# Hybrid decoder step on one Trainium2 core: the last two expert turns' rows added by TensorE, other rows combined while the experts run, rows dealt out over partitions

## What is computed

```python
m_in, mo_p, q1p, q2p, kr_p, vr_p = mixer_inputs(xp, norm_mix[l], w_in[l], b_gates[l])   # h @ w_in, gates among it
...
xp = xp + mixer_output(hm_p, mo_p, a_p, head_norm_m[l], head_norm_da[l], lam_init, w_out[l], xp.dtype)
...
# moe_ffn: the best of 4 groups, then the best 2 of its 8 experts
gates = jnp.sum(jax.nn.one_hot(expert_id, N_EXPERTS, dtype=jnp.float32) * top_p[..., None], axis=1)
y = jnp.zeros((N, h.shape[1]), jnp.float32)
for e in range(N_EXPERTS):
    act = jax.nn.silu(h @ w_gate[e]) * (h @ w_up[e])
    y = y + gates[:, e:e + 1] * (act @ w_down[e]).astype(jnp.float32)
...
y_prompt = rms_norm(xp, norm_final)[:, N_META:].astype(x_prompt.dtype)
y_sample = rms_norm(xs, norm_final).astype(x_sample.dtype)
```

## Time and profile before

| | us |
|---|---|
| median of 3 runs | 693.38 (692.94 to 696.12) |
| the profiled execution, its own time | 703.3 |
| its span, first to last instruction | 701.5 |
| TensorE busy | 611.1 (87%) |
| DVE busy | 279.6 (40%) |
| ScalarE busy | 139.2 (20%) |
| GpSimd busy | 116.4 (17%) |

### The profile page before, as it was taken

One profiled execution on the slowest core, in us unless ns is written; L12 is line 12 of the kernel. 1 busy time (PEld: TensorE's weight loads), 2 busy tenths in 40 slices (PEclk: granted clock), 3 DMA queues, 4 the chain that ended last, 5 costly groups with the idle time before them and its releaser, 6 DMA issues.

```text
span 701.5 us, 8557 instructions
## 1 busy us (share of the span) xinstructions
PE 611.1 (87%) x3155; PEld 328.6 (47%) x3155; DVE 279.6 (40%) x615; ACT 139.2 (20%) x405; POOL 116.4 (17%) x195
## 2 busy tenths in 40 slices
PE   4999999899898999999989996999999777999700
PEld 2444344445544555555545482555555443555300
DVE  3320068333333452568788778311212111121146
ACT  3111041233323454401131000110101100101111
POOL 2350016110040110101021201011121110211023
PEclk9999999999999999999999966999999998999965
DMA  9643337823030210041084798899999999999674
GB/s 282 197 142 135 121 102 207 280 83 118 4 106 15 73 48 0 1 121 62 1 327 156 238 407 328 359 419 419 419 420 421 419 422 421 420 420 415 250 262 166
DMA packets 49378, 161.45 MB, mean 230 GB/s; under 512 B 16443, under 2 KB 17772, under 8 KB 36664
## 3 DMA queue, kind: packets, MB, share of 16 engines
q1 hardware_dynamic: 39624, 143.67, 52.8%
q0 software_dynamic: 7488, 17.19, 7.4%
q10 hardware_dynamic: 2224, 0.04, 0.2%
HBM read 150.91 MB, written 19.01 MB: 242 GB/s over the span
## 4 chain that ended last, share of the span: by engine, by line
PE 68%; DMA 12%; SPq 7%; DVE 5%; ACT 3%; issue 2%; another core or an unknown queue 2%; POOL 1%; POOLq 0%; DVEq 0%; ACTq 0%
PE bank L1869 11%; PE bank L1872 11%; PE bank L2090 8%; PE bank_p L2140 6%; PE scores L2153 6%; DMA WS<-in_w_down_e 4%; DMA FT<-in_w_down_e 4%; PE bank_t L2140 4%; PE bank_t L1886 3%; SPq L552 3%; SPq L555 2%; DMA WS<-in_w_in 2%; SPq L549 2%; PE bank L2132 2%
## 5 line engine op out<-in xcount | busy, mean ns | idle before, releaser
L1872 PE MATMUL bank<-WS,XHT 128*128 128x512 f32 x192 | 87.4, 601 | 2.0 <-DMA WS<-in_w_in 1.5
L1869 PE MATMUL bank<-XHT,WS 128*128 128x512 f32 x192 | 85.0, 597 | 1.0 <-PE bank_t L1886 1.0
L1869 PEld LDWEIGHTS bank<-XHT,WS 128*128 128x128 f32 x192 | 35.7, 190 | 43.3 <-issue 43.0
L1872 PEld LDWEIGHTS bank<-WS,XHT 128*128 128x128 f32 x192 | 34.8, 190 | 42.5 <-issue 40.4
L2140 PE MATMUL bank_p<-WS,XHT 128*64 128x256 f32 x288 | 45.5, 391 | 5.7 <-DVE XHT L1724 1.5
L915 POOL DMA_INDIRECT out_rows<-MVA,slot_ids x17 | 17.0, 1001 | 188.1 <-DVE MVA L1741 188.1
L2140 PE MATMUL bank_t<-WS,XHT 128*64 128x256 f32 x288 | 43.0, 381 | 1.5 <-DMA FT<-in_w_up_e 0.8
L2140 PEld LDWEIGHTS bank_p<-WS,XHT 128*64 128x64 f32 x288 | 27.7, 141 | 21.0 <-issue 4.3
L1741 DVE COPY MVA<-scores 128x512 f32<-128x512 f32 x17 | 11.8, 692 | 56.9 <-PE scores L2153 56.9
L806 POOL TENSOR_SCALAR rr<-ss 128x1 f32<-128x1 f32 (+3 forms) x25 | 7.9, 316 | 158.7 <-ACT XHT L1145 46.3
L2140 PEld LDWEIGHTS bank_t<-WS,XHT 128*64 128x64 f32 x288 | 26.3, 137 | 15.6 <-DMA FT<-in_w_up_e 1.2
(11 more groups left out here) (427 smaller groups left out, 1022.6 us busy)
## 6 DMA issues: line engine op xcount, KB each, us to landing
WS<-in_w_gate_e SPq DMA_DIRECT2D x16, 1024.0 KB
WS<-in_w_up_e SPq DMA_DIRECT2D x16, 1024.0 KB
WS<-in_w_down_e SPq DMA_DIRECT2D x16, 1024.0 KB
WS<-in_w_in SPq DMA_DIRECT2D x6, 2048.0 KB, 11.8
XHT<-in_w_gate_e SPq DMA_DIRECT2D x10, 1024.0 KB
XHT<-in_w_up_e SPq DMA_DIRECT2D x10, 1024.0 KB
XHT<-in_w_down_e SPq DMA_DIRECT2D x10, 1024.0 KB
FT<-in_w_gate_e SPq DMA_DIRECT2D x6, 1024.0 KB
```

What stands on the lines that cost most here:

```text
L1869: mm = pe.matmul(PS[r][:, :], w[:, k, 128 * m:128 * (m + 1)], hT[:, k, 0:512], start=(k == 0), stop=(k == KC - 1))
L1872: mm = pe.matmul(PS[r][:, :], hT[:, k, 128 * m:128 * (m + 1)], w[:, k, :], start=(k == 0), stop=(k == KC - 1))
```

## The change

It has these parts:

- **Late rows by TensorE.** The results of the last two turns go to a DRAM tensor of their own, `end_rows`, and for the tiles 0 to 3 they are not read back. A matrix `chosen[k]` (128 rows of the turn by 512 tokens) holds the gate weight where row and token belong together; 16 products of `chosen` with `YO` (`late`) put the sums of both turns for all prompt tokens into PSUM, and DVE adds them (`add_late`).
- **Other rows earlier.** The tokens and the rows of turns 0 to 14 are loaded as soon as turn 14 is stored, into the buffers that its weights have left, and combined by `gather_early`. As rows of the last turns are absent from `out_rows`, it is filled with zeros first, in `mdec1`. Further turns, if there were more, write from `Yfar`.
- **Gate weights by slot.** `pw` is stored to DRAM as `pw_rows`, and GpSimd gathers the two columns of the last turns.
- **Spread samples.** The eight sample rows are combined as 128 rows of 64 elements (`gather_few`); masks made by GpSimd (`few_masks`) let TensorE spread their gate weights and sum their squares.
- **Dealt-out rows.** `riota` is permuted: consecutive ranks lie four partitions apart within groups of 32.
- **Split gates.** The gate projection takes its 512 tokens in two side-by-side products of 256, and ScalarE asks for `wg` at the block dq, 1.
- **Smaller ones.** Two constants are added to `eidx` and `piota` ahead of the routing; `pair_places` moves behind `rows_of(0)`; `rows_of` signals each half; the last turn's down product is copied by ScalarE alone; the tiles end with T4.

```diff
-LASTLY = (T4, 0, 1, 2, 3)
+LASTLY = (0, 1, 2, 3, T4)
...
+        out_rows, end_rows = dram("out_rows", (2 * SECOND, D)), dram("end_rows", (2 * SECOND, D))
+        pw_rows = dram("pw_rows", (2 * SECOND, 1))
...
+                return Sps[:, j - 2, 512 * half:512 * half + 512]
+            return (bank, (pt_, pp_))[j][half][:, :]
...
+                    sp.wait_ge(sel_made, 2)
+                    sp.dma_start(pw_rows.rearrange("(p r) a -> p (r a)", p=128), maskneg[:, 0:2 * SECOND // 128])\
+                      .then_inc(rows_zeroed, 16)
+                    for c in range(2):
+                        sp.dma_start(out_rows[SECOND * c:SECOND * c + SEQ].rearrange("(p r) (b d) -> p (r b) d", p=128, d=128),
+                                     maskneg[:, None, :].to_broadcast([128, 32, 128])).then_inc(rows_zeroed, 16)
+                        for rows in (out_rows, end_rows):
+                            sp.dma_start(spread(rows, SECOND * c + SEQ + S0), maskneg[:, 0:64]).then_inc(rows_zeroed, 16)
...
+                if n == NSETS + 1:
+                    sp.wait_ge(ids_ready, 2)
+                    sp.wait_ge(rows_zeroed, 16 * 7)
+                    for c in range(2):
+                        sp.dma_start(pw_rows[SECOND * c:SECOND * c + 128 * NTILES].rearrange("(j p) a -> p (j a)", p=128),
+                                     pw[:, c, :], allow_slow_non_contiguous=True).then_inc(pw_out, 16)
...
-            sp.wait_ge(dn_filled, LAST[PAIRS - 2] + 1)
-            for j in range(NTILES):
-                n = nrows(j)
-                sp.dma_start(X[0:n, j, :], x_rows[128 * j:128 * j + n]).then_inc(x_back[j], 16)
...
+            for b in range(NDEC):
+                sp.dma_start(gfew[16 * b:16 * b + 16], norm_final.rearrange("(s d) -> s d", d=64)).then_inc(gfin_in, 16)
+            sp.dma_start(XE[T4], spread(x_rows, SEQ + S0)).then_inc(x_back[T4], 16)
+
+            sp.wait_ge(dn_filled, LAST[PAIRS - 3] + 1)
+            for s in range(2):
+                sp.wait_ge(y_out[s], 16 * ((ENDING[0] + 1 - s) // 2))
+            for j in range(NT):
+                sp.dma_start(XE[j], x_rows[128 * j:128 * (j + 1)]).then_inc(x_back[j], 16)
+                for c in range(2):
+                    sp.dma_start(YG[j][:, c], out_rows[SECOND * c + 128 * j:SECOND * c + 128 * (j + 1)])\
+                      .then_inc((x_back, y_in)[c][j], 16)
...
-            src = out_rows.rearrange("(c t) d -> t c d", c=2)
-            for c in range(2):
-                sp.dma_start(YG[T4][S0:N4, c], src[SEQ + S0:SEQ + N4, c]).then_inc((x_back, y_in)[c][T4], 16)
-            for j in range(NT):
+            for n, rows in enumerate((out_rows, end_rows)):
                 for c in range(2):
-                    sp.dma_start(YG[j][:, c], src[128 * j:128 * (j + 1), c]).then_inc((x_back, y_in)[c][j], 16)
+                    sp.dma_start(Yfew[:, 2 * n + c], spread(rows, SECOND * c + SEQ + S0)).then_inc(y_in[T4], 16)
...
-            link(pool.iota(iscr[:, :], [[1, 128]], base=0, channel_multiplier=0))
+            link(pool.iota(iscr[:, :], [[32, 4], [1, 8], [8, 4]], base=0, channel_multiplier=0))
...
-                pool.indirect_dma_start(out_rows, bass.IndirectOffsetOnAxis(ap=slot_ids[:, c, 1:2].bitcast(u32), axis=0),
+                pool.indirect_dma_start(end_rows if i in ENDING else out_rows, bass.IndirectOffsetOnAxis(ap=slot_ids[:, c, 1:2].bitcast(u32), axis=0),
                                         YO[s], None, bounds_check=2 * SECOND - 1, oob_is_err=False).then_inc(y_out[s], 16)
...
+            def few_masks():
...
+                link(pool.memset(pick, 0.0))
+                link(pool.affine_select(out=blocks[0], in_=blocks[0], compare_op=ALU.not_equal, fill=1.0,
+                                        base=-S0, pattern=[[-1, NDEC], [0, 16]], channel_multiplier=1))
+                link(pool.iota(column_int, [[1, 512]], base=0, channel_multiplier=0))
+                link(pool.tensor_copy(column, column_int))
+                link(pool.memset(pw_end, 0.0))
+                pool.nop().then_inc(sel_made, 1)
+                pool.wait_ge(pw_out, 32)
+                for k, i in enumerate(ENDING):
+                    pool.indirect_dma_start(pw_end[:, k:k + 1], None, pw_rows,
+                                            bass.IndirectOffsetOnAxis(ap=slot_ids[:, TURNS[i][1], 1:2].bitcast(u32), axis=0),
+                                            bounds_check=2 * SECOND - 1, oob_is_err=False).then_inc(pw_in, 16)
...
+                pool.nop().then_inc(sel_made, 1)
...
+            pool.wait_ge(rows_zeroed, 16 * 7)
             for i in range(STATIC):
                 if i + 3 < STATIC:
                     fetch(i + 3)
                 store(i)
+                if i == 3:
+                    few_masks()
...
-            g = w_in[0].rearrange("(p k) n -> p k n", k=KC)[:, :, W_COLS["gates"]:W_COLS["gates"] + 8]
-            act.wait_ge(wg_zeroed, 1)
-            act.dma_start(wg[:, :, 0:H], g[:, :, 0:H]).then_inc(wg_in, 16)
-            act.dma_start(wg[:, :, 32:32 + H], g[:, :, H:2 * H]).then_inc(wg_in, 16)
...
+                    if (b, m) == ("dq", 1):
+                        g = w_in[0].rearrange("(p k) n -> p k n", k=KC)[:, :, W_COLS["gates"]:W_COLS["gates"] + 8]
+                        act.wait_ge(wg_zeroed, 1)
+                        act.dma_start(wg[:, :, 0:H], g[:, :, 0:H]).then_inc(wg_in, 16)
+                        act.dma_start(wg[:, :, 32:32 + H], g[:, :, H:2 * H]).then_inc(wg_in, 16)
...
+                if i == STATIC - 1:
+                    copy(YO[s][:, 512:1024], Sps[:, 0, 512:1024]).then_inc(y1, 1)
...
-                    link(v.scalar_tensor_tensor(early, eidx[:, None, 0:ne].to_broadcast([128, NTILES, ne]), float(SLOTS), early,
-                                                ALU.mult, ALU.add))
-                    link(v.tensor_scalar(early, early, float(-NOROOM), None, ALU.add))
+                    link(v.tensor_tensor(early, early, early_rows[:, None, :].to_broadcast([128, NTILES, ne]), ALU.add))
                     link(v.tensor_tensor(picked, m12[:, :, :, 0:ne], early[:, None].to_broadcast([128, 2, NTILES, ne]), ALU.mult))
                     link(v.tensor_reduce(slot_of, picked, AX.X, ALU.add))
-                    link(v.tensor_scalar(slot_of, slot_of, float(NOROOM), None, ALU.add))
-                    place_rows(first_onehots, piota[:, 0:EARLY])
+                    place_rows(first_onehots, early_pairs[:, :])
...
-                rows_in(xT[s]).then_inc(xt_evac, 1)
+                rows_in(xT[s])
...
+                dve.wait_ge(sel_made, 3)
+                dve.wait_ge(pw_in, 32)
+                for k, i in enumerate(ENDING):
+                    link(v.tensor_copy(id_end[:, k:k + 1], slot_ids[:, TURNS[i][1], 0:1]))
+                    v.tensor_scalar(chosen[k], column, id_end[:, k:k + 1], pw_end[:, k:k + 1],
+                                    ALU.is_equal, ALU.mult).then_inc(chosen_made, 1)
+
...
+            def gather_early(j):
+
+                dve.wait_ge(x_back[j], 32)
+                for c in range(2):
+                    if c:
+                        dve.wait_ge(y_in[j], 16)
+                    link(v.scalar_tensor_tensor(XE[j], YG[j][:, c], pw[:, c, j:j + 1], XE[j], ALU.mult, ALU.add))
+
+            def add_late(j):
+
+                dve.wait_ge(few_filled, j + 2)
+                if j < 2:
+                    for half in range(2):
+                        c = slice(512 * half, 512 * half + 512)
+                        ins = v.tensor_tensor(XE[j][:, c], XE[j][:, c], late_bank(j, half), ALU.add)
+                else:
+                    ins = v.tensor_tensor(XE[j], XE[j], Sps[:, j - 2, :], ALU.add)
+                ins.then_inc(x2_ready, 1)
...
             rows_of(0)
+            pair_places()
...
-            second_half(STATIC - 1)
+                if i == NSETS + 4:
+                    choose()
...
+            further(dve, further_blocks(dve), further_pair, stored=all_out)
+            gather_early(0)
+            gather_early(1)
+            add_late(0)
+            gather_early(2)
+            add_late(1)
+            finish(0)
+            gather_early(3)
+            add_late(2)
+            finish(1)
+            add_late(3)
+            gather_few()
+            for k in range(2, NTILES):
+                finish(k)
...
-                    for b, c0, c1_ in (("t", 0, 512), ("p", 512, TOK)):
-                        for k in range(KC):
-                            mm = pe.matmul(PS[b][0:36, 0:c1_ - c0], wg[:, k, :], hT[:, k, c0:c1_],
+                    for k in range(KC):
+                        for u in range(2):
+                            mm = pe.matmul(PS["t"][64 * u:64 * u + 36, 0:256], wg[:, k, :], hT[:, k, 256 * u:256 * u + 256],
                                            start=(k == 0), stop=(k == KC - 1))
-                        mm.then_inc(filled[b], 1)
+                    mm.then_inc(filled["t"], 1)
+                    for k in range(KC):
```

(29 more changed lines are left out.)

182 lines of the change are left out of this document (105 added, 77 removed).

## The result

| | before | after |
|---|---|---|
| median of 20 runs, us | 696.67 | 693.54 |
| ratio after / before | | 0.9944 (0.9922 to 0.9966) |
| profiled execution, own time / span | 703.3 / 701.5 | 690.7 / 688.8 |

The account below looks back on a forecast made before the run. Bounds: TensorE to about 430 us, the weight stream from 445 to 646, then a 35.7 us tail. Last weights at 653.5, TensorE's end 657.3, plus tail 29.9: span 687.2 (-14.3), scaled to -14.1 and 679.3 us; range 673.5 to 688.0.

Parts of the forecast that it names:

- (d): Gate weights stored to DRAM in 1,280 runs of 4 bytes in the full weight stream: +0.9 us (0 to 2).
- (b): Gate weights loaded later instead of at the start, ahead of the first weight block: -0.8 us (0 to 1.6).
- (a): Gate projection in the mixer split into two side-by-side products of 256 columns: -3.4 us (bounds 0 and 3.4).
- (f): Dealt-out rows load DMA engines evenly, so the weight stream ends earlier: -4.5 us (bounds 0 and -6.2).
- (e): Zero fill of 4.2 MB into the scatter buffers, done before SP's first expert load: 0 us (0 to +4).
- (g): Tail after TensorE's last down product: 29.9 us instead of 35.7, -5.8, with the scatter delaying the first root and DVE.
- T: End of TensorE's last down product, from which the tail is counted; forecast at 657.3 us.
- R1: Rival, tail: the last scatter lands in 9.8 us and holds the roots, tail 3.3 longer, 682.6 us; chance 0.12.
- R4: Rival, slower: the zero fill holds SP past 353, first six experts' weights come late, 697.7 us; chance 0.05.
- R2: Rival, tail: TensorE at its lower clock in the late products, 8.2 us more, 687.4 us; chance 0.09.
- R3: Rival: dealing changes nothing and the gates' 3.4 us are taken up by other waits, 687.1 us; chance 0.08.
- half evacuation: First rows' evacuation signalled by halves, so TensorE starts after 0.65 instead of 1.30 us in turn 0: -0.65 us.

Follow-up runs that it names:

- e3: Changed kernel with the gate projection as before (one 512-column product, its weights loaded at the start); ratio to the kernel before 0.9997.
- g2: Kernel before plus only the split gate projection with its weights asked for later; ratio to the kernel before 0.9921.
- e2: Changed kernel with rows filled in from the first on again, dealing undone; ratio to the kernel before 0.9995.
- g1: Kernel before plus only the dealt-out rows (permuted row numbers); ratio to the kernel before 0.9952.
- f4: On top of e1, SP instead of GpSimd waits for the last scatters, freeing GpSimd for the roots; ratio to the kernel before 0.9870.
- e1: Changed kernel with gate weights turned by a TensorE transpose and stored in ten runs of 512 bytes; ratio to the kernel before 0.9821.
- g3: Second measurement of the e1 kernel, nothing else changed; ratio to the kernel before 0.9844.
- h4: Third measurement of the e1 kernel, nothing else changed; ratio to the kernel before 0.9804.
- h3: The changed kernel measured once more, with no edit; ratio to the kernel before 0.9938.
- h2: Kernel before plus stores of the same 1,280 gate-weight numbers in 256 runs of 20 bytes; ratio to the kernel before 0.9999.
- g4: On top of e1, the four prompt tiles of x_rows not loaded again in the tail, residual left out; ratio to the kernel before 0.9806.

## Why the prediction was wrong

**(d) is the step that failed.** I priced 1,280 stores of 4 bytes at +0.9 us (0 to 2), from loads of 16 bytes at the start. Count and size of the runs were right. The price fits loads and separated stores (1.0 to 1.3 us of stream), but by luck, as the row from which I took it is not the gate loads' (see (b)). The nearest row was of the other direction, and the bound was no bound: nothing in the trace of before wrote neighbouring runs of 4 bytes into DRAM in a full stream. It cost 7.1 us of stream and 7 to 9 us of time.

**(b) rested on a wrong reading as well.** I took the 60 GB/s at 5 to 6 us for one of the gate loads. After, these loads are gone from the start, and the same window reads

```profile
5.00:6.00 1.00, 0.00 (x0) 0.00 (x0) 0.00 (x0) 0.89 (x3) 0.30 (x2) 1.00 0.66 55
```

Something else is slow there: over all eighteen traces this window has 27 to 95 GB/s, with the loads ahead of it or without. What they cost can be read from the start of the first weight block: 13.36 to 13.82 us in the eight traces with the loads at the start, 12.81 to 13.57 in the ten without, in the mean 13.63 and 13.23. So (b) was worth 0.4 us and not 0.8. It was small, and (a) and (b) together, forecast at 4.2, measured 3.5 (e3) and 5.5 (g2).

**(f) was right in mechanism, somewhat large in size:** -3.3 (e2) and -3.4 (g1) for -4.5; the stage says -3.1 to -3.9. The loss was the uneven load of the engines by packed rows (g1's edge). In g1 the weights were no longer what ended last: its second to last down product ran at a low clock and cost 1.4 us of the path (see the last section), and with these g1's stage would say -4.5. What I took from the Trainium skill, page "DMA: Bandwidth & Descriptors", section "The descriptor swizzle", -7.4, is twice what was measured; the direction agrees.

**(e) was right.** SP issues the last piece of the zero fill by 337.3 and its first expert load at 345.24, 7.8 us ahead of the earlier trace rows, like the work around it (the decode state's last load: 319.76 against 327.50), and the share from 328 to 353 rose from 0.11 to 0.71:

```profile
328.00:353.00 25.00, 23.17 (x90) 11.54 (x89) 18.88 (x46) 6.20 (x34) 5.76 (x8) 1.00 0.71 233
```

**(g) was right in size, for half of the reason.** The tail is 30.7, 30.6 and 29.6 us, forecast 29.9. The late products took 14.0 (13.8 forecast), the first root came 10.3 us after T as forecast and took 1.4 us (2.1 forecast), the first scaling at 12.3 (12.4). But the root did not hold DVE: f4 freed it and gained nothing. DVE was late by its waits for row loads, which I had at T + 6.5 and which lasted until T + 8.4 for the last tile it waited for (666.47 - 658.1); two equal delays hid each other. R1 did not happen, as the root's time shows, and R4 neither. R2 did not happen in the late products, whose clock was 1.00, but its mechanism did elsewhere (see the last section). R3's half (no effect of dealing and gates) is refuted by g2 for the gates, and by g1 and the stage of e2 for the dealing.

**The sum.** With the measured terms, in us: gates about -4.2, half evacuation -0.65 (not resolved by any run), stores +7 to +9, dealing -3.4, tail -5.3: -6.6 to -4.6, against -3.9 (-5.4 to -2.4) measured. The forecast of 14.1 less (d)'s 6 to 8, (f)'s 1.1 and (g)'s 0.5 is the same sum. It can be tested without (d): 14.1 and the 0.9 that I had charged, less (f)'s 1.1 and (g)'s 0.5, are 13.4, and e1, g3 and h4 gained 12.5, 10.9 and 13.6. What I left out of the range was a price that can be six times that of its nearest row.

## What to carry to other kernels

Don't write single 4-byte elements side by side into DRAM while a stream runs: 1,280 of them took 7 us from it, while the mean DMA share of the stretch stayed at 1.02. Turn them on TensorE into whole rows (here a transpose of 0.27 us and a copy of 0.25), or at least store several numbers of a partition together (20 bytes were enough here). And where a change's cost is bounded by the nearest row of the trace, ask whether that row has the same direction and the same neighbours; if not, the upper end is open, and a measurement of that one transfer is worth more than the rest of the sum.

## What was unexpected of the hardware

- The DMA share does not tell it: in the slump after had a share of 2.24 at 218 GB/s, of 1.06 at 49 and only then of 0.38 at 66. Only GB/s beside the share shows that engines are held up.
- Granted clock falls to 0.50, the lower of its two levels (1.2 GHz), for a few us in places that had none before. One is the first weight block of after (8.83 us for a block that took 7.13, granted clock 0.51 and 0.50 from 14 to 17 us). The other is the second to last down product. It took 5.1 to 5.4 us at a mean clock of 0.68 to 0.71 in eight of the eighteen traces (h3, g1, h2 and all five without the short stores: e1, g3, h4, f4, g4) and 3.65 at 1.00 in the ten others. In both groups TensorE had waited 1.7 to 2.6 us for a down load before it, so that the length of this wait does not tell them apart. After and e1 as examples:

```profile
649.37 3.65 PE L2277 MATMUL scores<-XHT,MK 128*64 128x512 f32 x16 [2.01 <-DMA XHT<-in_w_down_e]
654.41 0.61 PE L2277 MATMUL scores<-WS,FT 128*64 128x512 f32 x1 [0.95 <-DMA FT<-in_w_down_e]
```
```profile
643.20 5.35 PE L2281 MATMUL scores<-XHT,MK 128*64 128x512 f32 x16 [1.97 <-DMA XHT<-in_w_down_e]
649.53 0.62 PE L2281 MATMUL scores<-WS,FT 128*64 128x512 f32 x1 [0.55 <-ACT FT L1054]
```

Where the clock fell, the last down product starts 6.1 to 6.3 us behind the second to last instead of 4.9 to 5.1, and it waits for ScalarE's copy and not for the last weights: 1.2 to 1.4 us of the path go to R2's mechanism there. That before kept 1.00 with such pauses was one trace, too little for the weight that I gave it in the prediction.
